# Second attention of a two-block kernel: an output panel's halves made ahead, parts of four panels in the last round, and three steps of a round in another order

## The reference, cut to what matters

```python
def block_fn(args):                       # differential_attention, one block of queries
    q_blk, start = args
    ...
    logits = jnp.einsum('bqhjd,bkhjd->bhjqk', q_blk, k).astype(jnp.float32) + bias[None]
    p = jax.nn.softmax(logits, axis=-1)
    a = p[:, :, 0] - lam_full * p[:, :, 1]
    return jnp.einsum('bhqk,bkhe->bqhe', a.astype(v.dtype), v)

o = lax.map(block_fn, (qb, starts))
o = o.transpose(1, 0, 2, 3, 4).reshape(B, S, B_HEADS, 2 * HEAD_DIM)
o = rms_norm_2(o, subln_g) * (1.0 - lambda_init)
return o.reshape(B, S, B_HEADS * 2 * HEAD_DIM) @ w_o
```

## Time and profile before

| | |
|---|---|
| median of three runs | 3703.34 us (3700.42 to 3703.8) |
| profiled execution | 3701.99 us, span 3700.2 us |
| TensorE busy | 3569.7 us (96%) |
| VectorE busy | 2368.5 us (64%) |
| ScalarE busy | 1285.7 us (35%) |
| GpSimd busy | 1462.6 us (40%) |
| mean granted TensorE clock | 0.986 of full |
| chain that ended last | 86% of the span on TensorE |

### The profile page before, as it was taken

How to read it: one execution, slowest core, us unless ns; L and a number is a source line. 1 busy time by engine, 2 the same in 40 slices (tenths; PEclk the granted TensorE clock), 3 DMA queues, 4 the chain that set the end, 5 groups by cost and what they waited for, 6 DMA issues and landing times.

```text
span 3700.2 us, 48506 instructions
## 1 busy us (share of the span) xinstructions
PE 3569.7 (96%) x16414; PEld 2880.3 (78%) x16414; DVE 2368.5 (64%) x3750; ACT 1285.7 (35%) x1773; POOL 1462.6 (40%) x660
## 2 busy tenths in 40 slices
PE   6999999899999999999999999999999999889998
PEld 4777887788888888878888888775688888568886
DVE  5787897436666666358888887527584431668543
ACT  4555323334444444421111212336432232643221
POOL 2222443334343434344444444465144444124443
PEclk8999999999999999999999999989999999999999
DMA  5425322224454555585555653321122223212222
GB/s 209 154 96 189 123 93 80 91 83 133 142 188 154 184 159 170 184 264 191 190 189 200 202 188 123 104 79 51 50 96 97 97 99 103 85 45 97 97 97 85
DMA packets 267075, 486.58 MB, mean 132 GB/s; under 512 B 16769, under 2 KB 148225, under 8 KB 266657
## 3 DMA queue, kind: packets, MB, share of 16 engines
q1 hardware_dynamic: 90816, 304.12, 24.5%
q10 hardware_dynamic: 176132, 180.76, 14.9%
HBM read 415.48 MB, written 84.02 MB: 135 GB/s over the span
## 4 chain that ended last, share of the span: by engine, by line
PE 86%; DVE 6%; issue 4%; ACT 2%; DMA 1%; DVEq 0%; POOL 0%; ACTq 0%; SPq 0%; POOLq 0%
PE ps L380 25%; PE ps L382 25%; PE ps L381 25%; PE ps L606 3%; PE ps L709 2%; DVE ps L1682 1%; DMA ring<-panels 1%; PE ps L479 1%; PE ps L698 1%; PE ps L682 1%; DVE arena L1885 0%; ACT arena L1248 0%; PE ps L585 0%; ACT arena L1254 0%; DVE arena L1520 0%
## 5 line engine op out<-in xcount | busy, mean ns | idle before, releaser
L2045 POOL TENSOR_TENSOR ring_r<-ring,high_w 128x1024 fp32r<-128x1024 f32 x552 | 1363.2, 2471 | 2032.1 <-ACT high_w L822 1569.0
L380 PE MATMUL ps<-uT_r,high_w 128*128 128x512 f32 x2608 | 1034.9, 397 | 6.6 <-DVE part_x L1401 2.0
L382 PE MATMUL ps<-uT_r,ring_r 128*128 128x512 f32 x2608 | 1017.3, 390 | 0.0
L822 ACT ACTIVATE high_w<-ring 128x1024 fp32r<-128x1024 f32 x440 | 464.5, 1058 | 1219.3 <-PE ps L382 1071.5
L381 PE MATMUL ps<-sq_r,high_w 128*128 128x512 f32 x2032 | 791.0, 389 | 0.0
L381 PE MATMUL ps<-part,high_w 128*128 128x512 f32 x1840 | 718.4, 390 | 0.0
L380 PE MATMUL ps<-part,high_w 128*128 128x512 f32 x1664 | 651.3, 391 | 11.3 <-issue 5.4
L382 PE MATMUL ps<-part,ring_r 128*128 128x512 f32 x1664 | 649.5, 390 | 0.0
L380 PEld LDWEIGHTS ps<-uT_r,high_w 128*128 128x128 f32 x2608 | 491.4, 188 | 114.0 <-issue 9.9
L382 PEld LDWEIGHTS ps<-uT_r,ring_r 128*128 128x128 f32 x2608 | 491.0, 188 | 103.2
L1390 DVE SCALAR_TENSOR_TENSOR part<-arena 128x512 fp32r<-128x512 f32 x192 | 445.7, 2321 | 6.6
(11 more groups left out here) (328 smaller groups left out, 3709.6 us busy)
## 6 DMA issues: line engine op xcount, KB each, us to landing
ring<-panels SPq DMA_DIRECT2D x568, 512.0 KB, 3.4
gdram<-arena ACTq DMA_DIRECT2D x16, 2048.0 KB, 10.2
arena<-adram ACTq DMA_DIRECT2D x128, 256.0 KB, 2.7
adram<-act_out ACTq DMA_DIRECT2D x112, 256.0 KB, 3.8
arena<-gdram ACTq DMA_DIRECT2D x112, 256.0 KB, 4.7
arena<-ada_rest ACTq DMA_DIRECT2D x32, 512.0 KB, 4.3
strips_dram<-btab ACTq DMA_DIRECT2D x4, 3584.0 KB
arena<-strips_dram ACTq DMA_DIRECT2D x24, 448.0 KB, 3.3
```

The source lines that it names most:

```text
L380: t_.matmul(out, wh, xh, start=(k == 0), stop=False)
L382: last = t_.matmul(out, wl, xh, start=False, stop=(k == KT - 1))
L822: s_.activation(high_w[:, j % RING], ring[:, j % RING], ACT.Copy).then_inc(hi_ready, 1)
L2045: g_.tensor_tensor(ring_r[:, j], ring[:, j], high_w[:, j], ALU.subtract).then_inc(lo_ready, 1)
```

## The change

On PE: four output panels instead of three are done in parts. K-steps 0 to 4 of all four go into round 7, panels 0 and 1 at the end of its part 0, panels 2 and 3 at the end of its part 1. K-steps 5 and 6 follow behind `spread_b(6)`, with the statistic and the spreading of pair 7 behind panel 0's, and then the last k-step of each. `spread_b(n-2)` goes from the end of part 2 of a round to part 3, behind its two logits.

On ACT: `high` of output panel 3 goes ahead of round 0 (and is left out behind panel 0); `copied_b(n-1)` goes from behind exp e3 to behind exp e6 in rounds that have a next pair; `high_b(n-2)` goes from behind exp e7 to behind exp e6. On DVE: `out_b(n-2)` goes from behind unit e7 to behind unit e6. On POOL: `low` of output panel 3 goes ahead of all of the attention's own steps.

```diff
@@ -739,6 +739,10 @@
                                          start=True, stop=True)
                     last.then_inc(b_spread, 1)
 
+                def early_out(j):
+
+                    panel(q_wo, j, (kT_r, qT_r), ready=(a["oT_ready"], 0), ks=range(B_HEADS - 3))
+
                 def round_b(n):
 
                     for p in range(TT):
@@ -746,13 +750,16 @@
                             two_logits(n + 1, p)
                         if p == 0 and n >= 2:
                             bstat(n - 2)
+                        if p == 3 and n >= 2:
+                            spread_b(n - 2)
                         if p < 2 and n:
                             weighted(n - 1, 1 - n % 2, 0, n - 1, 2 * p)
                             weighted(n - 1, 1 - n % 2, 0, n - 1, 2 * p + 1)
                         for qt in ((), (0,), (1, 2), (3,))[p]:
                             turn(n % 2, 0, n, qt)
-                        if p == 2 and n >= 2:
-                            spread_b(n - 2)
+                        if n == B_HEADS - 1 and p in (0, 1):
+                            early_out(2 * p)
+                            early_out(2 * p + 1)
                     if n == B_HEADS - 1:
                         bstat(n - 1)
 
@@ -784,13 +791,13 @@
                     for kt in range(TT):
                         weighted(7, 1, 0, 7, kt)
                     spread_b(6)
-                    for j in range(3):
-                        panel(q_wo, j, (kT_r, qT_r), ready=(a["oT_ready"], 0), ks=range(KT - 1))
+                    for j in range(4):
+                        panel(q_wo, j, (kT_r, qT_r), ready=(a["oT_ready"], 0), ks=range(B_HEADS - 3, KT - 1))
                         if j == 0:
                             bstat(7)
                             spread_b(7)
                 for j in range(8):
-                    some = range(KT - 1, KT) if s and j < 3 else range(KT)
+                    some = range(KT - 1, KT) if s and j < 4 else range(KT)
                     panel(q_wo, j, (kT_r, qT_r), ready=None if j else (a["oT_ready"], 0), ks=some)
 
             attention(0, 3, Q_QKV_A, Q_WO_A)
@@ -864,7 +871,8 @@
 
                 for j in range(KT):
                     taken(q, j)
-                    high(q, j + 3)
+                    if r != 6 or j:
+                        high(q, j + 3)
                     if j:
                         if r in (2, 4, 5, 6):
                             high_of(3 if r == 2 else r, j - 1)
@@ -1288,11 +1296,11 @@
                             exp(n + 1, (n + 1) % 2, e % 2, e // 2, e)
                             if e >= 6 and n + 3 < B_HEADS:
                                 strips(2 * n + 6 + e % 2, e % 2)
-                        if e == TT - 1 and n:
+                        if e == (2 * TT - 2 if more else TT - 1) and n:
                             copied_b(n - 1)
                         if e >= TT - 1 and e < 2 * TT - 1:
                             turned(n % 2, n, e - TT + 1)
-                        if e == 2 * TT - 1 and n >= 2:
+                        if e == 2 * TT - 2 and n >= 2:
                             high_b(n - 2)
 
                 def quarters(i, c, more=True, fetch_more=True, old=True):
@@ -1338,6 +1346,7 @@
                         exp(0, 0, e % 2, e // 2, e)
                     strips(4, 0)
                     strips(5, 1)
+                    high(q_qkv + 3, 3)
                     for n in range(B_HEADS):
                         round_b(n)
                     copied_b(7)
@@ -2130,10 +2139,9 @@
             with po.Fori(0, at_b - at_a - 1) as i:
                 for j in range(RING):
                     low(i + (at_a + 1), j)
-            for j in range(RING - 1):
+            for j in range(RING):
                 low(at_b, j)
             second_attention()
-            low(at_b, RING - 1)
             with po.Fori(0, N_SPLIT // RING - at_b - 1) as i:
                 for j in range(RING):
                     low(i + (at_b + 1), j)
```

## The result

The changed kernel takes 3721.85 us (median of five runs, 3721.34 to 3723.5) against 3703.15 (five runs; the three at hand for the prediction had 3703.34); the ratio is 1.005, with a 95% interval from 1.0039 to 1.0061. The direction was as forecast; the size was not: +18.7 us where 11 were forecast, and 0.85 us above the range.

A forecast was written before the change was run, and what follows sets the result against it. TensorE, busy for 96% of the span, was taken as the bound, with a chain through several queues setting the attention's rounds. Rounds 3.9, start 2.1 and tail 5.0 summed to 11.0 us, forecasting 3714 us, range 3703 to 3721.

The forecast's parts named there:

- The new loop: In the attention's rounds, the next statistic waits for the moved square: 14.21 us a round against 13.57, +3.9 us in all.
- the loop through exp e7: In the rounds, a second loop through exp e7, behind the square and high_b, and the ratio: about the same length.
- the meeting of POOL and DVE: At the attention's start, POOL's subtraction for panel 3 holds DVE's second combination: +2.1 us, from 0 to 3.7.
- statistic 5 to spreading 6: Tail stage from pair 5's statistic to spreading of norm 6, with 60 early matmuls added: 27.8 us against 15.04.
- to spreading 7: Tail stage from pair 7's statistic to spreading of its norm, nothing new put under it: 3.38 us both times.
- to T: Tail stage from norm 7's spreading to panel 0's last k-step (T): 5.0 us against 10.54.
- The two waits that were new: In the tail, PE idles 2.3 us before k-step 6 and 5.2 us before output panel 4.
- the loss of the last round kept as it was: Low clock in the stretch after the last rounds' gaps, 0.89 on average: today's 1.65 us loss stays.
- 0.8 us in the middle of the tail: Low clock after the gaps of 2.3 and 2.5 us: none to 1.7 us, 0.8 taken.
- 1.7 us behind panel 4's start: After 5.2 us idle, output panel 4 starts at the lower clock level: +1.7 us.
- Rival (b): Clock also falls within the rounds, two or three times 1.7 us, beside a dear tail: 3720 or more; chance 0.10.
- Rival (a): Not slower: freed `turned` 0 and logits ahead of the spreading shorten the rounds, up to 1.16 us each; 3702 to 3705; chance 0.12.

The follow-up runs named there:

- e3: Not a run: a unit of a round in the second attention; ScalarE's exp e3 is the one the copy and square followed in the kernel before; no time of its own.
- square_back: The changed kernel with a pair's copy and square put back behind exp e3, all else as changed; 3709.28 us.
- order_only: The kernel before with spreading behind the last logits, scaling and high half behind e6; copy, square and panels as before; 3700.15 us.
- halves_only: The kernel before with only panel 3's halves made ahead of the pairs; 3702.24 us.
- best: order_only plus panel 3's high half in round 0 behind exp e5, and three k-steps of panel 1 before the last spreading; 3694.66 us.
- rounds_only: The kernel before with only the four moves inside a round (copy and square, high half, scaling, spreading), panels as before; 3710.14 us.

## Why the prediction was right in kind and too small in size

**The rounds.** What was worked out from the queues was right step by step. The new loop was worked out as 14.21 us and is 14.14; +0.57 a round, not 0.64. The prediction named what would be late next (the square ahead of the statistic) and said that the loop through exp e7 would be nearly as long; both waits are in the trace. square_back and order_only show that this one move is to blame: 12.91 us a round without it.

**The start.** +2.1 us by the meeting of POOL and DVE was forecast. The pair of combinations shows it (3.51 us), halves_only has 2.66 us by the statistic of pair 5, and best has none of it at another place. The Trainium skill (SBUF — State Buffer, Who interferes with whom) says that a DVE instruction with two SBUF inputs contends with a GpSimd instruction that reads SBUF. These traces agree: 3.51 us for the two combinations beside POOL, 1.41 without it.

**The tail's waits.** By the prediction's own stages, forecast against the changed kernel's trace: statistic 5 to spreading 6, 27.8 and 28.84; to statistic 7, 4.65 and 4.69; to spreading 7, 3.38 and 4.12; to T, 5.0 and 7.97; to panel 4, 7.95 and 7.85. The two waits that were new (2.3 forecast, 2.13 measured; 5.2 and 4.96) are right. The stages that came out longer (the first, the third and T) all follow an idle time of PE, of 2.36, 2.13 and 2.43 us.

**What failed: the price of the clock.** The sum had three terms for it: the loss of the last round kept as it was, 0.8 us in the middle of the tail, 1.7 us behind panel 4's start. Measured: two falls within the rounds, 3.3 us (15.78 and 15.79 less 14.14; 3.0 in rounds_only), where the sum had none; 3.0 us in the last round (24.44 less 21.41) where it kept 1.65; in the middle of the tail 0.74 and 2.97 us, 3.7 where it had 0.8; 2.0 us in panel 4 where it had 1.7. No row stood behind the 0.8: it was chosen between none and 1.7. By the stages, +3.0 in the rounds (6.9 for 3.9), +0.6 at the start, +4.7 in the five stages of the tail, of which 0.8 was in the sum, and +0.3 in panel 4 make 7.8, against the 7.7 that the forecast of 11.0 lacks to 18.7. The rounds' 6.9 are 2.9 for five rounds that are 0.57 us longer, 3.3 for the two falls and 0.7 ahead of the first statistic, which stays unexplained (rounds_only has 0.2 there). In the tail, the stages that are longer than the forecast are those at a low clock: 0.87 behind the statistic of pair 5, 0.50 from the statistic of pair 7 to its spreading, 0.62 from there to T, and 0.73 in panel 4. So nearly all of what was missing, but for the start's 0.6, is PE's clock. Rival (b) priced just this, but as a case by itself with a chance of 0.10, though its condition (two idle times close to each other in a round, much like the 0.78 and 1.71 us after which the clock had fallen in the earlier trace rows) followed from the forecast's own loop. It wasn't a rival but a term, and its own figure, 3720 or more, is what was measured. The range ended at 3721, at the lower edge of this rival, and so left out most of the case in which the rounds' falls and a dear tail come together, as they did.

That idle time sets off the low clock is shown: filling it gave back 5.0 and 3.9 us with the queues' order and the length of the rounds unchanged. The Trainium skill (TensorE: Matmul & The Clock Gate, A second HAM failure mode: psum-queue depth-cycling) tells of a kernel in which short idles between groups of matmuls made the clock go down and up again. The changed kernel's rounds agree in two of five, at a granted clock of 0.89.

**Rival (a)** was half right: three of the four moves do shorten the rounds, by 0.66 us a round together, but only with the fourth left out. The prediction had treated the moves as one edit and never asked what three of them would do.

**Open:** why the falls come in one round and not in the next with the same idle times, and after the same wait of 1.71 us in one execution and not in two others. Executions of one kernel differ by up to 6.5 us here, and no run was aimed at that. Also not tried: the changed kernel with both idle stretches filled at once.

## What to carry to other kernels

When a step is moved down a queue, ask what the next round waits for from it: here a square moved by three exps freed a copy at once and held TensorE one round later. Work pulled ahead of a wait is also work taken from behind the next one; look which load or chain it used to hide. And if a forecast adds TensorE idle time near that after which the clock fell in the same trace, the clock's loss belongs into the sum, not among the rivals.

## What the runs showed of the hardware

Matmuls that nobody reads made a kernel faster: 3716.9 against 3721.85 us with 24 more matmuls, of about 0.23 us each where they follow one another. The same matmuls of the panels start 0.23 us apart at full clock and 0.43 us apart from 3319.11 to 3321.67, where the clock is low. A POOL subtraction of 1024 elements a partition and two DVE combinations of two SBUF inputs cost DVE 2.1 us when they met, and POOL's record grew from 2.34 to 2.51 us; DVE's units, with one input from PSUM, weren't held by it (0.69 us in best). A DVE step on 128x4 elements took 1.24 us beside POOL's low half and 0.21 without it. A TensorE matmul ahead of which the view says "issue" was waiting for an activation that ended 0.10 us before it.
